# Sums of four squares written as a high and a low part and added by one-pass products, in three of the four openings of a decoder trunk

## The chip, the cores and the metric

The kernel runs on one core of a Trainium2 chip. The metric is the time of one execution on the device in microseconds. Three runs of the kernel before gave 2882.49, 2882.59 and 2882.88 us, so the median is 2882.59 us. The profiled execution is a fourth one; it took 2882.9 us by the same clock, of which 2881.1 us lie between its first and its last instruction (the span).

## The reference

It is a decoder trunk of two layers over 272 tokens (16 learned ones and 256 of the input) of width 2048, in float32. Every sub-layer is wrapped in two norms:

```
u = rmsnorm(h, pre_gain)
u = mixer(u)            # layer 0: sparse attention beside a gated delta rule; layer 1: retention
h = h + rmsnorm(u, post_gain)
u = swiglu(rmsnorm(h, ffn_pre_gain), w_gate, w_up, w_down)
h = h + rmsnorm(u, ffn_post_gain)
```

`rmsnorm(x)` is `x * rsqrt(mean(x*x) + 1e-6) * gain`, the mean taken over the 2048 channels of a token. There are eight norms, numbered 0 to 7 in the kernel. The even ones stand ahead of a large projection, the odd ones behind one. The change touches norms 2, 4 and 6.

## The kernel before, in words

Channels lie on the 128 partitions and in 16 chunks, tokens along the free axis, so `h` is 128 x 16 x 272. Norm 6 works on the 256 tokens behind the learned ones, the others here on all 272.

**Split products.** The kernel reaches float32 accuracy with one-pass products. Each weight and each activation is written as a high part (type fp32r) and a low part (the rest), and a tile of an output is 16 chunks times three products: high by high, low activation by high weight, high activation by low weight. ScalarE (ACT) writes the high parts (`w_hi`, `x_hi`), VectorE (DVE) subtracts them from the source to get the low parts (`w_lo`, `x_lo`; for norm 4 both lie in `ret_x`). SyncE (SP) issues the DMA loads of the weights. All matrix products go through the helper `mm`, which is why the profile gives nearly all of them line L647.

**An opening** is the start of the projection behind an even norm (stages up0, ret_in and up2 for norms 2, 4 and 6). The norm's factor is one number per token, so the products start on activations that aren't yet divided by the root; the root is applied when tiles leave PSUM. `fresh_three` computes the first three tiles together, chunk by chunk: for each chunk six products with `x_hi` and, one chunk later, three with `x_lo`. The fourth tile follows in `multiply`. TensorE waits for each chunk's `x_hi` and `x_lo` by semaphores, and for the first and second halves of each weight tile by `lo_ready`.

**What feeds it.** `h` itself is only finished in the opening. In `fill_x` of VectorE (L2280 and on) each pair of chunks goes through four steps in order: `x_low` of the pair (two instructions, L2333, from `h` and `x_hi`), `add_pair` of the pair after (L2348, one operand in PSUM), `scale_pair` (L2342, one operand in PSUM). Behind the last pair stand the first and second halves of the fourth tile's `w_lo` (L2325, 128x1024 each), the first half of the fifth tile's (L2258), and the reciprocal of the root (L2276). On ScalarE each pair gives two `x_hi` (L1599) and two squares (L1605); the squares of chunks 8 and on wait for `summed`, since their buffers are used again. The high part of the second half of the fourth tile's weights (L1552) waits until TensorE has passed the last pair of products of the second tile.

**The sum of squares.** In `square_fours` (L3122 and on) GpSimd (POOL) adds the squares in groups of four chunks, q = 0 to 3: chunk 0 + 1, chunk 2 + 3, and in `join` the two sums (three instructions, L3128). For q = 1 to 3 the join of the group before is held back until VectorE has written `x_lo` of chunk 4q + 1. The join of the last group has no such wait. TensorE adds the four results over partitions in `sum_four`: one float32 product with a matrix of ones, into one PSUM bank, behind chunks 7, 11 and 15 of `fresh_three` (sums 0, 1, 2) and behind chunk 3 of the fourth tile (sum 3). ScalarE then takes the root. The counters are `added` (POOL's additions), `summed` (sums done), `x_lo_ready`.

GpSimd's program from norm 1 on is: a running sum of squares for norm 1, half of a weight split, norm 2's fours, norm 3's sum, a weight split, norm 4's fours, the DMA of `rel`, the copy of the ones to fp32r (`ones_ret`, used in the retention), the retention's work, then norm 5's sum, a split and norm 6's fours.

The same high-and-low way of summing exists elsewhere in the kernel: in the delta rule (L3192 to L3203, with `ones_two`) and in the retention (L3294, L3296 and the products with `ones_ret`).

Of the kernel before, what the change touches and what calls it, by code (L numbers as in the profile page):

```python
# [28 lines left out]
ALU = mybir.AluOpType  # L29
AX = mybir.AxisListType  # L30

P = 128
D = 2048
META = 16
SEQ = 256
T = META + SEQ
KC = D // P
# [45 lines left out]

def added_after(norm, q, op):

    return 12 * (norm // 2) + 3 * q + op + 1  # L90
# [87 lines left out]
def trunk(nc, a, out):  # L178
    ctx = ExitStack()
    st = stage_table()  # L180
    with ctx:
        def sb(name, shape, dt=F32, c=ctx):
            return c.enter_context(nc.sbuf_tensor(name, shape, dt))

        def sem(name):
            return ctx.enter_context(nc.semaphore(name))
# [27 lines left out]
        ones = sb("ones", [P, P])  # L214
# [56 lines left out]
        with ExitStack() as second:  # L271
            with ExitStack() as whole:
                mid = sb("mid", [P, 64 * SEQ], F32R, whole)
# [20 lines left out]
            ones_ret = sb("ones_ret", [P, P], F32R, second)  # L294

        mid_hi = mid[:, 0:32 * SEQ]
        mid_lo = mid[:, 32 * SEQ:64 * SEQ]

        def mid_at(layer, low, j):

            if layer == 0:
                return 640 * j + (288 if low else 0)
            return (32 * SEQ + 32 if low else 64) + j * SEQ
# [15 lines left out]
        one_col = ones[:, 0:1]  # L319
# [53 lines left out]
        ps = ctx.enter_context(nc.psum_tensor("ps", [P, 8, 512], F32))  # L373
        BK_SUM, BK_D0, BK_D1, BK_0, BK_1, BK_2, BK_3 = 2, 2, 3, 4, 5, 6, 7
# [25 lines left out]
        x_lo_ready = sem("x_lo_ready")  # L400
        squared = sem("squared")
        added = sem("added")
        summed = sem("summed")
        rooted = sem("rooted")
        r_ready = sem("r_ready")
# [232 lines left out]
        def square_slot(norm, k):  # L638
            if norm == 0:
                return q_index[:, k % 8]  # L640
            return [ffn_g, ffn_m, k_rot, rot_a][k // 2 % 4][:, k % 2, FROM[norm]:T]
# [3 lines left out]
        def _(pe):  # L645
            def mm(o, lhs, rhs, start, stop):
                return nc.tensor.matmul(o, lhs, rhs, start=start, stop=stop)  # L647
# [69 lines left out]
            def fresh_pair(base):  # L717

                behind, t0 = 2, FROM[0]
                for k in range(KC + behind):  # L720
                    j = k - behind
                    if k < KC:
                        if k in (0, 4):
                            pe.wait_ge(first_lo, k // 2 + 1)
                        if k == 8:
                            pe.wait_ge(lo_ready, 2 * base + 2)
                        fresh_hi(0, k, t0)
                        half = fresh_lo(0, k, t0)
                        if k in (7, KC - 1):
                            half.then_inc(products, 1)  # L730
                    if k in (10, 14):
                        if k == 10:
                            pe.wait_ge(ones_in, 16)
                        sum_four(0, k // 4 - 2)
                    if j >= 0:
                        if j in (0, 4):
                            pe.wait_ge(first_lo, j // 2 + 2)
                        if j == 8:
                            pe.wait_ge(lo_ready, 2 * (base + 1) + 2)
                        last = multiply(ps[:, BK_1, t0:T], 1, j, 1, lambda _: x_hi[:, j, t0:T],  # L740
                                        lambda _: x_lo[:, j, t0:T], j == 0, j == KC - 1)
                last.then_inc(products, 2)

            def fresh_three(stage, norm, t0):
# [4 lines left out]
                for k in range(KC + 1):  # L749
                    j = k - 1  # L750
                    if k < KC:
                        if k == 8:
                            pe.wait_ge(lo_ready, 2 * base + 2)
                        fresh_hi(norm, k, t0)
                        if k % 8 == 0:
                            pe.wait_ge(lo_ready, 2 * (base + 1) + 1 + k // 8)
                        cut, high = slice(k * P, (k + 1) * P), x_of(x_hi, t0, norm)[:, k]
                        mm(second, w_hi[:, 1, cut], high, k == 0, False)
                        mm(second, w_lo[:, 1, cut], high, False, False)
                        if k == 0:  # L760
                            pe.wait_ge(third_lo_ready, 2 * THIRD.index(stage) + 2)
                        mm(third, third_hi[:, cut], high, k == 0, False)
                        mm(third, third_lo[:, cut], high, False, False)
                    if j >= 0:
                        fresh_lo(norm, j, t0)
                        cut, low = slice(j * P, (j + 1) * P), x_of(x_lo, t0, norm)[:, j]
                        pair = mm(second, w_hi[:, 1, cut], low, False, j == KC - 1)
                        if j == 7:
                            pair.then_inc(products, 1)
                        elif j == KC - 1:  # L770
                            pair.then_inc(products, 3)
                        last = mm(third, third_hi[:, cut], low, False, j == KC - 1)
                    if k in (7, 11, 15):
                        sum_four(norm, k // 4 - 1)
                last.then_inc(products, 2)

            def sum_four(norm, q):

                t0 = FROM[norm]
                if q == 0 and norm:  # L780
                    pe.wait_ge(r_ready, norm)
                pe.wait_ge(added, added_after(norm, q, 2))
                mm(ps[:, BK_SUM, t0:T], ones[:], square_slot(norm, 4 * q), q == 0, q == 3).then_inc(summed, 4)

            def sum_behind(norm):

                def behind(k):
                    if k == 3:
                        sum_four(norm, 3)
                return behind  # L790
# [2315 lines left out]
        def _(pool):  # L3106
            G = nc.gpsimd
# [15 lines left out]
            def square_fours(norm):  # L3123

                t0 = FROM[norm]

                def add(q, to, other):
                    G.tensor_tensor(square_slot(norm, 4 * q + to), square_slot(norm, 4 * q + to),  # L3128
                                    square_slot(norm, 4 * q + other), ALU.add).then_inc(added, 1)

                def join(q):
                    pool.wait_ge(added, added_after(norm, q, 1))
                    add(q, 0, 2)

                for q in range(4):
                    if q:

                        pool.wait_ge(x_lo_ready, KC * (norm // 2) + 4 * q + 2)
                        join(q - 1)
                    pool.wait_ge(squared, KC * norm + 4 * q + 2)  # L3140
                    add(q, 0, 1)
                    pool.wait_ge(squared, KC * norm + 4 * q + 4)
                    add(q, 2, 3)
                join(3)

            square_fours(0)

            for t in range(8):
# [95 lines left out]
            def square_sum(norm):  # L3244

                t0 = FROM[norm]

                def add(k, slot):
                    pool.wait_ge(squared, KC * norm + k + 1)
                    if isinstance(k, int) and k == 0:  # L3250
                        G.tensor_copy(sq_sum[:, t0:T], sq[:, slot, t0:T]).then_inc(summed, 1)
                    else:
                        pool.wait_ge(summed, KC * norm + k)
                        G.tensor_tensor(sq_sum[:, t0:T], sq_sum[:, t0:T], sq[:, slot, t0:T], ALU.add
                                        ).then_inc(summed, 1)

                add(0, 0)
                add(1, 1)
                with pool.Fori(1, KC // 2 - 1) as i:
                    for s in range(2):  # L3260
                        add(2 * i + s, s)

            def split_second(stage):

                piece = st[stage][0] + 1
                cut = slice(HALF_W, FULL)
                pool.wait_ge(hi_ready, 2 * piece + 2)
                pool.wait_ge(lo_ready, 2 * piece + 1)
                G.tensor_tensor(w_lo[:, 1, cut], raw[:, 1, cut], w_hi[:, 1, cut], ALU.subtract).then_inc(lo_ready, 1)

            square_sum(1)
            split_second("up0")
            square_fours(2)
            square_sum(3)
            split_second("ret_in")
            square_fours(4)
            _, sig, tile0 = st["ret_in"]
            pool.wait_ge(products, sig + 6)
            pool.dma_start(rel, a["rel"]).then_inc(rel_in, 16)
            G.tensor_copy(ones_ret[:], ones[:])  # L3280

            def ret_round(i):

# [116 lines left out]
```

## Time and profile before

| | value |
|---|---|
| median of three runs | 2882.59 us |
| profiled execution | 2882.9 us |
| its span | 2881.1 us |
| TensorE busy | 2854.4 us (99%) |
| VectorE busy | 1695.1 us (59%) |
| ScalarE busy | 1370.4 us (48%) |
| GpSimd busy | 244.0 us (8%) |
| opening of norm 2 | about 559 to 587 us |
| opening of norm 4 | about 1360 to 1387 us |
| opening of norm 6 | about 2147 to 2174 us |

The profile calls TensorE's products PE, its weight loads PEld. A row of the timeline has the start, the duration, the engine, the line, the operation, what is written and read, and how many like instructions were merged into it; brackets at its end give the idle time before it and who ended it. Products are pipelined, so what one costs TensorE is read from the distance of the starts and not from its duration.

### The profile page before, as it was taken

How to read it: one execution, taken by the hardware profiler on the slowest of the kernel's cores; microseconds unless marked ns; L12 is line 12 of the kernel's file. 1: busy time of each engine (PE TensorE's matmuls, PEld its weight loads, DVE VectorE, ACT ScalarE, POOL GpSimd, SP SyncE). 2: the span in 40 equal slices, each digit the busy share in tenths (PEclk: the TensorE clock that was granted, in tenths of full speed). 3: DMA queues.
4: the chain of work that ended last, by engine and by line, in shares of the span. 5: the costliest groups of instructions: out<-in, count | busy, mean ns of one | idle time of the engine just before them, and what ended most of it. 6: DMA issues, size and time to landing. Idle time of an engine off the chain costs nothing.

```text
span 2881.1 us, 58384 instructions
## 1 busy us (share of the span) xinstructions
PE 2854.4 (99%) x22720; PEld 2786.5 (97%) x22720; DVE 1695.1 (59%) x2402; ACT 1370.4 (48%) x1997; POOL 244.0 (8%) x273
## 2 busy tenths in 40 slices
PE   9999999999999999999999999999999999999998
PEld 8989999999999999999999999999999998899987
DVE  5887775755554455545655555555466556555555
ACT  5556665643343333345544444444454444344443
POOL 2222110300000000001211111110010000000000
PEclk9999999999999999999999999999999999999999
DMA  5222334444445544455344444444544555555554
GB/s 214 103 98 88 124 105 140 165 154 174 175 165 176 188 174 175 179 173 195 130 167 175 163 170 162 175 162 173 218 175 161 196 192 202 197 189 192 192 200 161
DMA packets 74823, 483.89 MB, mean 168 GB/s; under 512 B 8989, under 2 KB 9417, under 8 KB 24432
## 3 DMA queue, kind: packets, MB, share of 16 engines
q1 hardware_dynamic: 74528, 482.30, 47.2%
q8 instruction: 59, 0.97, 0.1%
q0 software_dynamic: 208, 0.39, 0.0%
q14 instruction: 28, 0.23, 0.0%
HBM read 480.41 MB, written 2.10 MB: 167 GB/s over the span
## 4 chain that ended last, share of the span: by engine, by line
PE 94%; DVE 4%; ACT 1%; issue 1%; DMA 0%; SPq 0%; POOL 0%; DVEq 0%; ACTq 0%
PE ps L647 93%; DVE w_lo L2258 0%; DVE w_lo L2406 0%; PE ps L1039 0%; DVE x_lo L2333 0%; DVE conv_acc L2435 0%; PE ps L1442 0%; DMA h<-in_x_t 0%; DVE ps L2342 0%; DVE h L2348 0%; DMA raw<-in_w_heads 0%; DVE bias L2537 0%; DVE r_pre L2276 0%; ACT w_hi L2002 0%; PE ps L947 0%
## 5 line engine op out<-in xcount | busy, mean ns | idle before, releaser
L2258 DVE TENSOR_TENSOR w_lo<-raw,w_hi 128x1024 fp32r<-128x1024 f32 (+2 forms) x885 | 1001.8, 1166 | 371.9 <-ACT w_hi L1520 357.8
L1520 ACT ACTIVATE w_hi<-raw 128x1024 fp32r<-128x1024 f32 (+2 forms) x835 | 822.9, 1012 | 519.3 <-PE ps L647 447.9
L647 PE MATMUL ps<-x_hi,w_hi 128*128 128x272 f32 (+1 forms) x3424 | 985.0, 288 | 7.4 <-ACT x_hi L1599 4.1
L647 PE MATMUL ps<-x_hi,w_lo 128*128 128x272 f32 (+1 forms) x3424 | 968.9, 283 | 0.2 <-DVE u L2672 0.2
L647 PE MATMUL ps<-x_lo,w_hi 128*128 128x272 f32 (+1 forms) x3424 | 963.8, 283 | 1.8 <-DVE x_lo L2333 1.8
L647 PEld LDWEIGHTS ps<-x_hi,w_hi 128*128 128x128 f32 x3424 | 645.4, 188 | 11.9 <-issue 4.6
L647 PEld LDWEIGHTS ps<-x_lo,w_hi 128*128 128x128 f32 x3424 | 643.3, 188 | 4.2 <-DVE x_lo L2333 2.9
L647 PEld LDWEIGHTS ps<-x_hi,w_lo 128*128 128x128 f32 x3424 | 642.3, 188 | 0.6 <-DVE u L2672 0.5
L647 PE MATMUL ps<-ret_x,w_hi 128*128 128x272 f32 (+1 forms) x3040 | 557.4, 284 | 1.5 <-ACT ret_x L1599 1.1
L647 PEld LDWEIGHTS ps<-ret_x,w_hi 128*128 128x128 f32 x3040 | 469.8, 188 | 2.4 <-ACT ret_x L1599 1.1
L647 PE MATMUL ps<-mid,w_hi 128*128 128x272 f32 (+1 forms) x2432 | 437.0, 282 | 0.0
L647 PE MATMUL ps<-ret_x,w_lo 128*128 128x272 f32 (+1 forms) x1520 | 429.7, 283 | 0.0
L647 PEld LDWEIGHTS ps<-mid,w_hi 128*128 128x128 f32 x2432 | 374.4, 188 | 0.0
L647 PE MATMUL ps<-mid,w_lo 128*128 128x272 f32 (+1 forms) x1216 | 342.7, 282 | 0.0
L647 PEld LDWEIGHTS ps<-ret_x,w_lo 128*128 128x128 f32 x1520 | 286.2, 188 | 0.0
L647 PEld LDWEIGHTS ps<-mid,w_lo 128*128 128x128 f32 x1216 | 228.0, 188 | 0.0
L647 PE MATMUL ps<-w_hi,mid 128*128 128x512 f32 x704 | 218.9, 392 | 0.0
L2145 ACT ACTIVATE mid<-ffn_m 128x272 f32 (+3 forms) x88 | 37.3, 424 | 342.0 <-DVE ffn_m L3001 342.0
L647 PEld LDWEIGHTS ps<-w_hi,mid 128*128 128x128 f32 x704 | 132.0, 188 | 29.5
L2159 ACT ACTIVATE ffn_g<-ffn_g 128x272 f32<-128x272 f32 (+1 forms) x88 | 37.3, 424 | 229.5 <-DVE ffn_g L2987 229.5
L647 PE MATMUL ps<-w_lo,mid 128*128 128x512 f32 x352 | 138.5, 393 | 0.0
L2997 DVE TENSOR_TENSOR ffn_m<-ps,r_pre 128x272 f32<-128x272 f32 (+1 forms) x88 | 38.0, 432 | 125.4 <-PE ps L647 125.4
(381 smaller groups left out, 2660.0 us busy)
## 6 DMA issues: line engine op xcount, KB each, us to landing
raw<-in_w_up SPq DMA_DIRECT2D x172, 1024.0 KB, 4.8
raw<-in_w_ret_in SPq DMA_DIRECT2D x94, 1024.0 KB, 4.8
raw<-in_w_down SPq DMA_DIRECT2D x64, 704.0 KB, 4.0
raw<-in_w_rows SPq DMA_DIRECT2D x44, 1024.0 KB, 4.8
raw<-in_w_heads SPq DMA_DIRECT2D x32, 1024.0 KB, 4.8
raw<-in_w_ret_out SPq DMA_DIRECT2D x32, 1024.0 KB, 4.8
raw<-in_w_mix_early SPq DMA_DIRECT2D x16, 768.0 KB, 4.3
raw<-in_w_latent SPq DMA_DIRECT2D x6, 1024.0 KB, 4.8
```

The lines of the kernel that those rows point to most:

```text
L647: return nc.tensor.matmul(o, lhs, rhs, start=start, stop=stop)
L1520: nc.scalar.activation(w_hi[:, piece % 2, cut], raw[:, piece % 2, cut], ACT.Copy).then_inc(hi_ready, count)
L2145: nc.scalar.activation(mid[:, bass.ds(mid_at(layer, False, j), w)], ffn_m[:, slot, 0:w], ACT.Copy).then_inc(mid_hi_ready, 1)
L2159: nc.scalar.activation(ffn_g[:, s, 0:w], ffn_g[:, s, 0:w], ACT.Silu).then_inc(gate_silu, 1)
L2258: V.tensor_tensor(w_lo[:, slot, cut], raw[:, slot, cut], w_hi[:, slot, cut], ALU.subtract).then_inc(lo_ready, count)
L2997: V.tensor_tensor(ffn_m[:, s, 0:w], ps[:, up_bank, t0:T], r_pre[:, t0:T], ALU.mult).then_inc(drained, 1)
```

## The change

For norms 2, 4 and 6 GpSimd writes two more instructions behind each join: the high part of the sum (`four_hi`, a multiplication by a column of ones into type fp32r) and the low part (`four_lo`, the sum less the high part). One pair of buffers serves all four groups, so from the second group on the high part waits until TensorE's sum of the group before is done. TensorE waits for both parts in place of the join (`fours_parted` in place of `added`), and adds two one-pass products in place of one float32 product. The copy of the ones to `ones_ret` moves ahead of norm 2's fours. Norm 0 stays as it was.

```diff
+def parted_after(norm, q, low):
+    return 8 * (norm // 2 - 1) + 2 * q + low + 1
@@
+        four_hi, four_lo = mid[:, 48 * SEQ:48 * SEQ + T], mid[:, 50 * SEQ:50 * SEQ + T]
@@
+        fours_parted = sem("fours_parted")
@@ sum_four (TensorE)
                 if q == 0 and norm:
                     pe.wait_ge(r_ready, norm)
-                pe.wait_ge(added, added_after(norm, q, 2))
-                mm(ps[:, BK_SUM, t0:T], ones[:], square_slot(norm, 4 * q), q == 0, q == 3).then_inc(summed, 4)
+                if norm == 0:
+                    pe.wait_ge(added, added_after(norm, q, 2))
+                    mm(ps[:, BK_SUM, t0:T], ones[:], square_slot(norm, 4 * q), q == 0, q == 3).then_inc(summed, 4)
+                    return
+                pe.wait_ge(fours_parted, parted_after(norm, q, 1))
+                mm(ps[:, BK_SUM, t0:T], ones_ret[:], four_hi[:, 0:T - t0], q == 0, False)
+                mm(ps[:, BK_SUM, t0:T], ones_ret[:], four_lo[:, 0:T - t0], False, q == 3
+                   ).then_inc(summed, 4)
@@ join, in square_fours (GpSimd)
                 def join(q):
                     pool.wait_ge(added, added_after(norm, q, 1))
                     add(q, 0, 2)
+                    if norm:
+                        total, high = square_slot(norm, 4 * q), four_hi[:, 0:T - t0]
+                        pool.wait_ge(added, added_after(norm, q, 2))
+                        if q:
+                            pool.wait_ge(summed, KC * norm + 4 * q)
+                        G.tensor_tensor(high, total, one_col.to_broadcast([P, T - t0]), ALU.mult
+                                        ).then_inc(fours_parted, 1)
+                        pool.wait_ge(fours_parted, parted_after(norm, q, 0))
+                        G.tensor_tensor(four_lo[:, 0:T - t0], total, high, ALU.subtract
+                                        ).then_inc(fours_parted, 1)
@@ GpSimd's program
             split_second("up0")
+            G.tensor_copy(ones_ret[:], ones[:])
             square_fours(2)
@@
             pool.dma_start(rel, a["rel"]).then_inc(rel_in, 16)
-            G.tensor_copy(ones_ret[:], ones[:])
```

## Rows read from the trace of the kernel before

**Rows 1.** The page: busy shares, TensorE's granted clock in 40 slices.
```profile
PE 2854.4 (99%) x22720; PEld 2786.5 (97%) x22720; DVE 1695.1 (59%) x2402; ACT 1370.4 (48%) x1997; POOL 244.0 (8%) x273
PEclk9999999999999999999999999999999999999999
```

**Rows 2.** TensorE's waits: norm 2's opening, then a later one in norm 4's.
```profile
564.83 0.39 PE L647 MATMUL ps<-x_hi,w_hi 128*128 128x272 f32 x1 [1.08 <-ACT x_hi L1599]
...
1393.82 0.49 PE L647 MATMUL ps<-ret_x,w_hi 128*128 128x272 f32 x2 [0.41 <-DVE k_rot L3076]
```

**Rows 3.** Timeline of TensorE, norm 2: sum 0 and two products behind it.
```profile
569.49 0.62 PE L647 MATMUL ps<-ffn_g,ones 128*128 128x272 f32 x2
569.75 0.49 PE L647 MATMUL ps<-x_hi,w_hi 128*128 128x272 f32 x1
570.08 0.29 PE L647 MATMUL ps<-x_hi,w_lo 128*128 128x272 f32 x1
570.20 0.29 PE L647 MATMUL ps<-x_hi,w_hi 128*128 128x272 f32 x1
```

**Rows 4.** Timeline of TensorE: a pair of one-pass products, in the retention.
```profile
1434.44 0.41 PE L647 MATMUL ps<-ret_x,ones_ret 128*128 128x256 f32 x2
1434.68 0.40 PE L647 MATMUL ps<-ret_x,w_hi 128*128 128x256 f32 x2
```

**Rows 5.** Timeline of TensorE: sum 2 of norm 2, sum 3 of norms 2 and 6.
```profile
579.46 0.62 PE L647 MATMUL ps<-ffn_g,ones 128*128 128x272 f32 x2
...
581.79 0.62 PE L647 MATMUL ps<-k_rot,ones 128*128 128x272 f32 x2
...
2167.88 0.59 PE L647 MATMUL ps<-k_rot,ones 128*128 128x256 f32 x2
```

**Rows 6.** GpSimd's high and low parts elsewhere: nanoseconds, minimum/median/maximum.
```profile
L3201 POOL TENSOR_TENSOR third_hi<-u,ones x7: 639/640/1857, 155.4 to 422.2; 128x272 fp32r<-128x272 f32 x7
L3203 POOL TENSOR_TENSOR third_hi<-u,third_hi x7: 663/663/727, 157.3 to 422.9; 128x272 fp32r<-128x272 f32 x7
L3296 POOL TENSOR_TENSOR ret_x<-ret_sq,ret_x x8: 741/741/743, 1433.1 to 1960.3; 128x256 fp32r<-128x256 f32 x8
```

**Rows 7.** Timeline of GpSimd, norm 2: first addition, joins 0 and 2, last addition, join 3.
```profile
560.35 0.96 POOL L3128 TENSOR_TENSOR ffn_g<-ffn_g 128x272 f32<-128x272 f32 x1 [1.32 <-ACT ffn_g L1605]
...
565.95 0.76 POOL L3128 TENSOR_TENSOR ffn_g<-ffn_g,ffn_m 128x272 f32<-128x272 f32 x1 [2.66 <-DVE x_lo L2333]
...
575.49 0.78 POOL L3128 TENSOR_TENSOR ffn_g<-ffn_g,ffn_m 128x272 f32<-128x272 f32 x1 [1.72 <-DVE x_lo L2333]
...
577.74 1.75 POOL L3128 TENSOR_TENSOR rot_a<-rot_a 128x272 f32<-128x272 f32 x1 [0.73 <-ACT rot_a L1605]
579.57 0.76 POOL L3128 TENSOR_TENSOR k_rot<-k_rot,rot_a 128x272 f32<-128x272 f32 x1
```

**Rows 8.** Timeline of VectorE, norm 2: chunks 6 and 7, then the end.
```profile
567.24 0.92 DVE L2333 SCALAR_TENSOR_TENSOR x_lo<-h,gains,x_hi 128x272 fp32r<-128x272 f32 x2
...
576.63 1.09 DVE L2333 SCALAR_TENSOR_TENSOR x_lo<-h,gains,x_hi 128x272 fp32r<-128x272 f32 x2 [0.59 <-ACT x_hi L1599]
577.64 1.21 DVE L2325 TENSOR_TENSOR w_lo<-fourth_raw,w_hi 128x1024 fp32r<-128x1024 f32 x1
581.46 1.23 DVE L2325 TENSOR_TENSOR w_lo<-fourth_raw,w_hi 128x1024 fp32r<-128x1024 f32 x1 [2.60 <-ACT w_hi L1552]
582.60 1.22 DVE L2258 TENSOR_TENSOR w_lo<-raw,w_hi 128x1024 fp32r<-128x1024 f32 x1
```

**Rows 9.** GpSimd and VectorE side by side in the retention.
```profile
1389.56 1.64 POOL L3287 TENSOR_TENSOR q_rot<-rot_a,q_rot 128x256 f32<-128x256 f32 x1 [7.49 <-DVE q_rot L3076]
1391.16 1.72 POOL L3288 TENSOR_TENSOR q_rot<-rot_a,q_rot 128x256 f32<-128x256 f32 x1
...
1389.39 2.89 DVE L2258 TENSOR_TENSOR w_lo<-raw,w_hi 128x1024 fp32r<-128x1024 f32 x2
```

**Rows 10.** GpSimd's DMA of `rel`: size, microseconds from issue to landing.
```profile
h_rows<-in_rel POOLq DMA_DIRECT2D x1, 232.0 KB, 3.1
```

## The prediction, as put on record before the change was run

> **What bounds the kernel now.** I read the page first. TensorE is busy 99% of the span at the full granted clock, GpSimd 8% [rows 1]. So what TensorE is spared comes off the time, and what it is made to wait goes on it. Then I listed its waits. In norm 2's opening there is one of 1.08 us, for `x_hi` of chunk 4, long before the sums that change; behind the openings one matters here, 0.41 us in norm 4's, for a drained tile [rows 2]. Then I laid the engines' timelines side by side in the three openings. They have the same order of instructions three times; the rows shown are norm 2's, and I walk that one.
>
> The profiled execution took 2882.9 us (span 2881.1, 1.8 around it). Its time is 0.3 above the median of 2882.59; I add my sum to the median.
>
> **TensorE's part.** Sum 0 starts at 569.49, the product behind the next one at 570.08, and plain products follow each other by 0.12 to 0.13 [rows 3]. So a float32 sum costs 0.59 - 0.125 = 0.465 us. A pair of one-pass products is in the retention: from its start to the next, 0.24 us for 256 columns [rows 4], taken as 0.25 for 272. Saved: 0.21 in each of 8 sums, and in norm 6's four some 0.19 (its sum's row is 0.03 shorter [rows 5]): together **-2.4 us**. This is the lower bound of everything else, since nothing else is removed.
>
> **GpSimd's part.** Each of 12 joins gets a high part, 0.64 us undisturbed, and a low part, 0.66 to 0.74 [rows 6]; with 0.08 us for each wait on its own result (join 3 starts 0.08 behind the addition that ended at 579.49 [rows 7]) that is 1.5 us. Sums 0 to 2 can carry it: join 0 ends at 566.71, sum 0 is at 569.49; join 2 ends at 576.27, sum 2 is at 579.46 [rows 3, 5, 7]. Sum 3 is another matter. Join 3 ends at 580.33 and TensorE comes at 581.79 [rows 5, 7], 1.46 us later, and at 581.16 once three sums are cheaper. Ahead of join 3 now stand three more pairs of instructions, of which the third is in the chain: join 2 is held to 575.49 by `x_lo` of chunk 13, and from there GpSimd runs nearly without a pause.
>
> **The port.** What decides is how long GpSimd's instructions take there. The addition at 577.74 took 1.75 us, its neighbours 0.76 [rows 7]. VectorE ran a 128x1024 split from 577.64 to 578.85 [rows 8], and the addition ended 0.64 behind it. The retention shows the rule in full: two such splits start at 1389.39, GpSimd's instruction of 1389.56 ends at 1391.20, the next at 1392.88, and the two splits together take 2.89 us instead of some 2.35 [rows 9]. First split to 1390.53, GpSimd 0.66, second split to 1392.28, GpSimd 0.60. So a GpSimd instruction and a VectorE instruction with two operands in SBUF exclude each other, one instruction at a time, in turn. The rows of `x_lo` (two operands in SBUF) obey it; the ones with an operand in PSUM don't: join 0, at 565.95, took its plain 0.76 us beside one. From these rows, a held GpSimd instruction ends 0.64 (addition) or 0.60 (low part) behind its rival, I take 0.52 for the high part; a held `x_lo` ends 0.30, a held split 1.08 behind.
>
> The Trainium skill speaks here against the change: its GPSIMD Engine Reference (section 1, Specifications) has GpSimd's SBUF interfaces shared with VectorE, with contention where VectorE's instruction has two SBUF inputs. The trace agrees, and adds the turns.
>
> **The walk, norm 2.** Join 0 to 566.72, high part to 567.44. `x_lo` of chunk 6 is issued at 567.24 [rows 8], held, done 567.74; low part to 568.34; `x_lo` 7 to 568.64 instead of 568.16. VectorE is 0.5 late; `h`, and so `x_hi` of chunk 8, too: TensorE waits 0.1 to 0.2 and has lost what sum 0 saved. The same at join 1, another 0.1 late or less, with sum 1's gain spent. Join 2 is released near 576.05. Its high part ends at 577.54, `x_lo` 14 at 577.84, low part 578.44, `x_lo` 15 578.74 (before 577.72), the first of the last two additions 579.38, the split that ran at 577.64 ends at 580.46, second addition 581.10. Sum 2 at TensorE is at 579.5 as before; the fourth tile starts some 0.2 late.
>
> Join 3: 581.18 to 581.94. The next split was issued at 581.46, behind a `w_hi` that ScalarE writes once TensorE is past sum 2, so it keeps its place; it waits for the join and ends at 583.02. High part to 583.54. The fifth tile's split, issued behind it [rows 8], to 584.62. Low part to **585.22**. TensorE wants sum 3 at some 582.0, starts at 585.27 and is through at 585.52, where before it was at 581.79 + 0.465 = 582.25: **+3.3 us**, which holds the savings of all four sums.
>
> The same walk gives +4.0 in norm 4, since its first low part comes just ahead of `x_lo` 6 and holds both chunks, so that TensorE waits 0.8 at chunk 8 and keeps that delay; less the 0.4 us wait behind it [rows 2], which vanishes (root and drains are late by less than TensorE): +3.6. In norm 6 the sum is over at 2171.7, before at 2167.88 + 0.43 = 2168.3 [rows 5]: +3.4. **Sum: +10.3 us.**
>
> **Bounds of the walk.** If VectorE isn't pushed back before join 3, join 3 is at 580.33 to 581.08, the high part done by 581.80, ahead of the split; that ends at 582.88, low part 583.48, sum over at 583.78: +1.5 per opening, 4.1 in all after the 0.4. If join 3 falls just behind the split's start, the end moves by half a microsecond: +3.9 per opening, +11.5 in all. I take the walk, because the turns reproduce each stretched row to 0.05 us.
>
> **The rest.** The copy of the ones moves into the 1.32 us in which GpSimd waited ahead of norm 2's fours [rows 7]: nothing. The DMA of `rel` goes out some 5 us later and lands 3.1 us after [rows 10], still ahead of its reader in the retention, which is behind the late root: nothing; without that cover the two or three microseconds would be ScalarE's. The wait on `summed` is met each time: sum 2 is over near 580, its buffers are written at 583. The root waits for sum 3 but stood behind two of ScalarE's splits before, so it is late by less than TensorE itself, and the drains that it releases keep their place. No queue of SyncE is passed.
>
> **Rivals.**
> A, *late, but little*: GpSimd's high part of sum 3 gets in ahead of the split. For it: join 3 is ahead of it now by 0.8 us. Against: the walk eats that. +4.1: 2886.7. Chance 0.17.
> B, *all hidden*: the low part of sum 3 is there by 581.2. Against: even with undisturbed durations the eight instructions from join 2's release at 575.49 on, 6.1 us with their waits, end at 581.6. -2.4: 2880.2, the other side of the zero. It decides only if GpSimd gets through them in 5.7 us. Chance 0.06.
> C, *the clock falls too*: a wait of 3.3 us between full stretches isn't in this trace, the granted clock is full in all 40 slices [rows 1]; the longest wait of these openings, 1.08 us [rows 2], left it full. If it halved for the rest of the fourth tile (36 products by 0.125 = 4.5 us), each opening would cost 4.5 more, +23.8: 2906. Chance 0.05. The Trainium skill bears on it (TensorE: Matmul & The Clock Gate, Why this matters for your kernels): it advises against idle gaps between bursts of products, since the clock drops behind them. By it the time would be C's 2906; the trace agrees as far as waits of 1.08 us go, which left the clock full, and shows none of 3 us here.
> D, *one opening of three as in A*, or a pair of one-pass products as dear as the float32 one (+2.4): between 2888 and 2896, inside my range.
>
> **The numbers.** This kernel's runs can tell about 0.2%, 5.8 us, from no change. Forecast 2882.6 + 10.3 = **2892.9** (with D, chance 0.72; its own range 2888.5 to 2895.5). A and B lie within 0.2%, together 0.23, and 0.02 of the walk's low end too; C counts as slower. Slower 0.73, same 0.25, faster 0.02 (only beyond what is removed). The range takes in most of A: 2885.5 to 2895.5, leaving out B, C and the tails, 0.2.
>
> **What would show it.** TensorE's first one-pass product of sum 3 waits 3 us or more on GpSimd in each of three openings; GpSimd's high and low parts there take 1.5 us each and more; pairs of `x_lo` at chunks 6 and 10 take 1.4 us instead of 0.92; the three splits behind them are 1 us or more late; norm 4's wait of 0.41 is gone. Wrong if sum 3's wait is under 2 us (A), absent (B), or if the clock's row shows less than 9 in slice 9, 20 or 31 (C).

## The result, and the profile after

Five runs of the changed kernel gave 2897.00 to 2899.05 us, median 2897.68; the kernel before gave a median of 2882.53 beside them. The ratio is 1.0052, with a 95% interval of 1.0042 to 1.0063: **15.1 us slower**, where 10.3 were forecast. The profiled execution took 2897.7 us (span 2895.8, 14.7 more than before). Helpers moved down, so L647 is now L654, `x_lo` is L2346, the two kinds of `w_lo` L2338 and L2271, GpSimd's additions L3141; its high part is L3152 and its low part L3155.

The page, busy shares and the clock in 40 slices:

```profile
PE 2858.5 (99%) x22720; PEld 2789.1 (96%) x22720; DVE 1705.4 (59%) x2402; ACT 1370.9 (47%) x1997; POOL 267.7 (9%) x297
...
PEclk9999999999999999999999999999999999999999
```

Against [rows 1] almost nothing has moved: GpSimd has its 24 instructions and 24 us more. TensorE's waits, grouped by who released them (us in total, times, longest), say where the time is:

```profile
PE ps L654 <- POOL mid L3155: 8.8, 3, 3.0
PE ps L654 <- ACT x_hi L1612: 4.8, 8, 1.1
PE ps L654 <- ACT ret_x L1612: 2.1, 3, 1.0
```

The first line is new: one wait in each opening for the low part of sum 3. In the same view of before, the next two were 4.1 (6 times) and 1.1 (twice): 1.7 us more, for the high parts of activations. Norm 2 has one more such wait, of 0.85 us, ahead of chunk 12, and norm 4 one of 0.97 us, ahead of chunk 8 (right behind sum 0); in norm 6 none of this size is new. The wait for `k_rot` of [rows 2] is gone. Norm 2's opening, TensorE's sums and waits, then norm 4's sum 0 and the wait behind it:

```profile
569.48 0.41 PE L654 MATMUL ps<-mid,ones_ret 128*128 128x272 f32 x2
574.61 0.41 PE L654 MATMUL ps<-mid,ones_ret 128*128 128x272 f32 x2
575.86 0.39 PE L654 MATMUL ps<-x_hi,w_hi 128*128 128x272 f32 x1 [0.85 <-ACT x_hi L1612]
580.51 0.41 PE L654 MATMUL ps<-mid,ones_ret 128*128 128x272 f32 x2
581.56 0.36 PE L654 MATMUL ps<-x_hi,w_hi 128*128 128x272 f32 x1 [0.26 <-DVE w_lo L2338]
586.22 0.51 PE L654 MATMUL ps<-mid,ones_ret 128*128 128x272 f32 x2 [2.92 <-POOL mid L3155]
...
1374.17 0.41 PE L654 MATMUL ps<-mid,ones_ret 128*128 128x272 f32 x2
1375.55 0.36 PE L654 MATMUL ps<-ret_x,w_hi 128*128 128x272 f32 x1 [0.97 <-ACT ret_x L1612]
```

Sum 0 of norm 2 stands where it stood [rows 3]; sum 2 is 1.05 us late and sum 3 is 4.43 late [rows 5]. GpSimd in the same stretch (joins 1, 2 and 3 with what follows them):

```profile
571.04 0.77 POOL L3141 TENSOR_TENSOR k_rot<-k_rot,rot_a 128x272 f32<-128x272 f32 x1 [0.99 <-DVE x_lo L2346]
571.89 0.64 POOL L3152 TENSOR_TENSOR mid<-k_rot,ones 128x272 fp32r<-128x272 f32 x1
572.61 0.77 POOL L3155 TENSOR_TENSOR mid<-k_rot,mid 128x272 fp32r<-128x272 f32 x1
573.34 0.98 POOL L3141 TENSOR_TENSOR ffn_g<-ffn_g 128x272 f32<-128x272 f32 x1
...
576.98 0.77 POOL L3141 TENSOR_TENSOR ffn_g<-ffn_g,ffn_m 128x272 f32<-128x272 f32 x1 [1.73 <-DVE x_lo L2346]
...
580.29 1.74 POOL L3141 TENSOR_TENSOR rot_a<-rot_a 128x272 f32<-128x272 f32 x1
582.12 0.78 POOL L3141 TENSOR_TENSOR k_rot<-k_rot,rot_a 128x272 f32<-128x272 f32 x1
582.97 1.50 POOL L3152 TENSOR_TENSOR mid<-k_rot,ones 128x272 fp32r<-128x272 f32 x1
584.55 1.62 POOL L3155 TENSOR_TENSOR mid<-k_rot,mid 128x272 fp32r<-128x272 f32 x1
```

And VectorE, chunks 6 and 7, then 10 and 11, then the splits:

```profile
567.25 1.44 DVE L2346 SCALAR_TENSOR_TENSOR x_lo<-h,gains,x_hi 128x272 fp32r<-128x272 f32 x2
...
572.11 0.73 DVE L2355 TENSOR_TENSOR ps<-u,ps 128x544 f32<-128x544 f32 x1 [0.51 <-DVE h L2361]
572.74 1.88 DVE L2346 SCALAR_TENSOR_TENSOR x_lo<-h,gains,x_hi 128x272 fp32r<-128x272 f32 x2
...
582.31 1.67 DVE L2338 TENSOR_TENSOR w_lo<-fourth_raw,w_hi 128x1024 fp32r<-128x1024 f32 x1 [0.90 <-ACT w_hi L1565]
583.90 1.66 DVE L2271 TENSOR_TENSOR w_lo<-raw,w_hi 128x1024 fp32r<-128x1024 f32 x1
```

The turns are there. The split issued at 582.31 waits for join 3 (to 582.90) and ends at 583.98; the high part waits for it and ends at 584.47; the next split waits for that and ends at 585.56; the low part waits for that and ends at 586.17. Only then does TensorE start. Undisturbed, high and low part take 0.64 and 0.77 (571.89 and 572.61); here they take 1.50 and 1.62.

At sum 3 the other openings show the same turns, and one thing more. Norm 4's last sum and the products behind it, then the stretches of the windows view (window and its length, then busy time and count of PE, PEld, DVE, ACT and POOL; then the granted clock, DMA's share, GB/s):

```profile
1390.95 0.82 PE L654 MATMUL ps<-mid,ones_ret 128*128 128x272 f32 x2 [2.98 <-POOL mid L3155]
1391.57 0.65 PE L654 MATMUL ps<-ret_x,w_hi 128*128 128x272 f32 x2
1392.02 0.43 PE L654 MATMUL ps<-ret_x,w_lo 128*128 128x272 f32 x1
...
1394.06 0.31 PE L654 MATMUL ps<-ret_x,w_lo 128*128 128x272 f32 x1
```

```profile
586.00:589.00 3.00, 2.78 (x22) 2.78 (x23) 1.70 (x1) 1.77 (x2) 0.17 (x1) 1.00 0.00 0
1390.00:1391.00 1.00, 0.05 (x1) 0.06 (x1) 0.28 (x1) 0.00 (x0) 1.00 (x2) 0.84 0.00 0
1391.00:1394.00 3.00, 3.00 (x13) 3.00 (x14) 1.67 (x1) 0.49 (x1) 0.46 (x1) 0.50 0.34 85
1394.00:1395.00 1.00, 1.00 (x10) 1.00 (x9) 0.96 (x3) 0.51 (x1) 0.00 (x0) 0.95 0.00 0
...
2181.00:2184.00 3.00, 2.92 (x19) 2.92 (x20) 1.83 (x2) 1.76 (x2) 0.03 (x1) 0.76 0.00 0
2184.00:2186.00 2.00, 2.00 (x11) 2.00 (x11) 1.97 (x4) 1.37 (x2) 0.00 (x0) 0.50 0.00 0
```

The granted clock is at its lower level (1.2 instead of 2.4 GHz) for 0.32 + 3 + 0.1 = 3.4 us behind the wait of 2.98 us in norm 4, and again for 1.4 + 2 = 3.4 us in norm 6, where the fall comes about 1.5 us after the products are back from a wait of 2.93 us. Behind norm 2's wait of 2.92 us it stays full. A stretch of 3.4 us at half speed does the work of 1.7 us, so each costs **1.7 us**, 3.4 in this execution. The clock's row of the page can't show it: a slice there is 72 us.

**Where the 14.7 us are**, by the first product of each opening. Norm 4's first product comes at 1364.22, before at 1359.90; norm 6's at 2156.22, before at 2146.80:

```profile
1364.22 0.36 PE L654 MATMUL ps<-ret_x,w_hi 128*128 128x272 f32 x1 [0.22 <-ACT ret_x L1612]
...
2156.22 0.36 PE L654 MATMUL ps<-x_hi,w_hi 128*128 128x256 f32 x1 [0.33 <-ACT x_hi L1612]
...
2181.08 0.51 PE L654 MATMUL ps<-mid,ones_ret 128*128 128x256 f32 x2 [2.93 <-POOL mid L3155]
```

So norm 2 cost 4.3, norm 4 5.1 and norm 6 the remaining 5.3. Less the clock, 4.3 + 3.4 + 3.6 = 11.3 us.

### The profile page after: what moved, and what is told of

The parts are those of the page before. It is cut to its first block, busy times and chain, and to the rows that moved or that the text cites. A ratio compares the mean times of both kernels' runs of the same rounds, so it can differ in the third digit from the quotient of the medians.

```text
span 2895.8 us, 58408 instructions
## 1 busy us (share of the span) xinstructions
PE 2858.5 (99%) x22720; PEld 2789.1 (96%) x22720; DVE 1705.4 (59%) x2402; ACT 1370.9 (47%) x1997; POOL 267.7 (9%) x297
## 4 chain that ended last, share of the span: by engine, by line
PE 92%; DVE 3%; POOL 2%; ACT 1%; issue 1%; DMA 0%; SPq 0%; POOLq 0%; DVEq 0%; ACTq 0%
PE ps L654 91%; POOL mid L3155 0%; POOL mid L3152 0%; POOL k_rot L3141 0%; DVE w_lo L2419 0%; DVE x_lo L2346 0%; DVE ps L2355 0%; DVE w_lo L2271 0%; PE ps L1052 0%; POOL rot_a L3141 0%; POOL ffn_g L3141 0%; DVE conv_acc L2448 0%; PE ps L1455 0%; DMA h<-in_x_t 0%; DVE h L2361 0%
## 5 line engine op out<-in xcount | busy, mean ns | idle before, releaser
L2271 DVE TENSOR_TENSOR w_lo<-raw,w_hi 128x1024 fp32r<-128x1024 f32 (+2 forms) x885 | 1003.0, 1168 | 369.6 <-ACT w_hi L1533 355.6
L654 PE MATMUL ps<-x_hi,w_hi 128*128 128x272 f32 (+1 forms) x3424 | 985.3, 288 | 8.8 <-ACT x_hi L1612 4.8
L654 PE MATMUL ps<-x_hi,w_lo 128*128 128x272 f32 (+1 forms) x3424 | 969.7, 284 | 0.2 <-DVE u L2685 0.2
L654 PE MATMUL ps<-x_lo,w_hi 128*128 128x272 f32 (+1 forms) x3424 | 964.3, 283 | 1.5 <-DVE x_lo L2346 1.5
L654 PEld LDWEIGHTS ps<-x_hi,w_hi 128*128 128x128 f32 x3424 | 646.1, 189 | 14.4 <-issue 5.7
L654 PEld LDWEIGHTS ps<-x_lo,w_hi 128*128 128x128 f32 x3424 | 643.9, 189 | 3.8 <-DVE x_lo L2346 2.8
L654 PEld LDWEIGHTS ps<-x_hi,w_lo 128*128 128x128 f32 x3424 | 643.1, 188 | 0.5 <-DVE u L2685 0.5
L654 PE MATMUL ps<-ret_x,w_hi 128*128 128x272 f32 (+1 forms) x3040 | 557.9, 284 | 2.3 <-ACT ret_x L1612 2.1
L654 PEld LDWEIGHTS ps<-ret_x,w_hi 128*128 128x128 f32 x3040 | 470.7, 189 | 3.3 <-issue 1.5
L654 PE MATMUL ps<-mid,w_hi 128*128 128x272 f32 (+1 forms) x2432 | 437.0, 282 | 0.0
L654 PE MATMUL ps<-ret_x,w_lo 128*128 128x272 f32 (+1 forms) x1520 | 430.1, 283 | 0.0
L654 PEld LDWEIGHTS ps<-mid,w_hi 128*128 128x128 f32 x2432 | 374.3, 188 | 0.0
L654 PE MATMUL ps<-mid,w_lo 128*128 128x272 f32 (+1 forms) x1216 | 342.7, 282 | 0.0
L654 PEld LDWEIGHTS ps<-ret_x,w_lo 128*128 128x128 f32 x1520 | 286.8, 189 | 0.0
L654 PEld LDWEIGHTS ps<-mid,w_lo 128*128 128x128 f32 x1216 | 228.0, 188 | 0.0
L654 PE MATMUL ps<-w_hi,mid 128*128 128x512 f32 x704 | 218.9, 392 | 0.0
L654 PEld LDWEIGHTS ps<-w_hi,mid 128*128 128x128 f32 x704 | 132.0, 188 | 29.5
L654 PE MATMUL ps<-w_lo,mid 128*128 128x512 f32 x352 | 138.5, 393 | 0.0
```

Source lines behind the costliest of these rows:

```text
L2271: V.tensor_tensor(w_lo[:, slot, cut], raw[:, slot, cut], w_hi[:, slot, cut], ALU.subtract).then_inc(lo_ready, count)
```

## The experiments

All ratios are to the kernel before on the same chip, whose medians there were 2882.53 (e1 to e4), 2882.83 (e5 to e8) and 2882.84 us (e9, e10). The 95% intervals reach some 0.1% (2.6 us) to either side, so those of e2, e4, e6, e8 and e9 reach "no change". The repeats lie closer together than that: e4's slowest run (2881.18) is under the fastest of the kernel before (2882.01), and the lowest runs of e6 and e8 (2883.80 and 2884.94) are over its median beside them. Differences under about 0.5 us are not read. In the cuts of the edits the counting of the semaphores, which follows each edit, is left out. My theory: the turns between GpSimd and VectorE push sum 3's parts behind the splits. Rivals: GpSimd simply has too many instructions, the new wait or the one-pass products are what costs, or the clock does.

### e1: only sums 0 to 2 parted

```diff
@@ sum_four
-                if norm == 0:
+                if norm == 0 or q == 3:
@@ join
-                    if norm:
+                    if norm and q < 3:
```

> High and low parts and one-pass products for sums 0, 1 and 2 only; sum 3 of each opening as before. Theory (turns at the port, chain in front of sum 3): VectorE's x_lo of chunks 6, 7, 10, 11 are pushed as in the changed kernel (1.44 and 1.88 us a pair in norm 2's opening in place of 0.92 and 0.91), so TensorE is still late at chunk 12 and the fourth tile still begins 1.3 us late (581.56 in place of 580.29); join 3 ends near 582.9, just ahead of TensorE's 583.1, so no wait of more than 0.2 us on GpSimd, and the clock stays full. Sum over three openings: +1.3, +0.8, +0.7, so +2.8 us (2885.3). Rival (the whole loss is the wait at sum 3 and the clock behind it; the parts ahead cost TensorE nothing): three sums cheaper in three openings, -1.8 us (2880.7).

Measured 2885.86 us, ratio 1.0011 (1.0002 to 1.002): **+3.3**. TensorE waits 0.85 us at chunk 12, as in the changed kernel, and join 3 starts 12.6 us behind sum 0 (581.53, 568.90), as there: the parts of sum 3 have no share in join 3's lateness. The theory said +2.8, the rival -1.8.

### e2: only sum 3 parted

```diff
-                if norm == 0:
+                if norm == 0 or q < 3:
@@ join
-                    if norm:
+                    if norm and q == 3:
```

> High and low part and one-pass products for sum 3 only; sums 0 to 2 as before. Theory (turns): VectorE is not pushed before join 3; join 3 to 581.08, high part 581.80, VectorE's split behind it to 582.88, low part 583.48, so TensorE waits 1.7 us at sum 3 and each opening costs +1.5, less the 0.4 wait that vanishes in norm 4's: +4.1 us (2886.7); the clock stays full behind waits of 1.7 us. Rival (only the length of the chain counts, no exclusion): low part at 582.6, +0.6 per opening, +1.5 in all (2884.1).

Measured 2882.59 us, ratio 1.0 (0.9991 to 1.0009): **no change**; the expectation missed. GpSimd, then VectorE's split:

```profile
579.04 0.77 POOL L3141 TENSOR_TENSOR k_rot<-k_rot,rot_a 128x272 f32<-128x272 f32 x1
579.89 0.64 POOL L3150 TENSOR_TENSOR mid<-k_rot,ones 128x272 fp32r<-128x272 f32 x1
580.61 0.77 POOL L3153 TENSOR_TENSOR mid<-k_rot,mid 128x272 fp32r<-128x272 f32 x1
```

```profile
580.90 1.56 DVE L2338 TENSOR_TENSOR w_lo<-fourth_raw,w_hi 128x1024 fp32r<-128x1024 f32 x1 [2.57 <-ACT w_hi L1565]
```

Join 3 ends at 579.81, both its parts are done at 581.38, and TensorE takes the sum at 581.43. This time the split waits for GpSimd (it ends at 582.46, 1.08 behind the low part) and not the other way round. The bound had read 580.33, the *end* of join 3 in [rows 7], as its start. Sum 3's parts alone cost nothing; they cost when earlier pairs have pushed join 3 into the splits.

### e3: GpSimd writes the parts of groups 0 to 2, TensorE doesn't use them

The float32 products stay; TensorE waits for the parts as in e1.

```diff
@@ sum_four
-                if norm == 0:
+                if norm >= 0:
+                    if norm and q < 3:
+                        pe.wait_ge(fours_parted, parted_after(norm, q, 1))
                     pe.wait_ge(added, added_after(norm, q, 2))
@@ join
-                    if norm:
+                    if norm and q < 3:
```

> GpSimd writes the parts of groups 0, 1 and 2, but TensorE adds the sum itself by one float32 product as before (it waits for the parts, which are early). Theory (turns): the loss of the parts ahead of sum 3 is VectorE's, not TensorE's, and TensorE is bound by x_hi of chunks 8 and 12 and by the split of the fourth tile; so nearly the time of the kernel with the cheaper sums, at most 0.6 us more per opening: +3 to +4.5 us (2885.5 to 2887). Rival (GpSimd's added work is free until sum 3): +0.0 (2882.5).

Measured 2885.87 us, ratio 1.0011 (1.0002 to 1.002): **+3.3**, the same as e1. In norm 2 TensorE waits 0.65 us at chunk 12 instead of e1's 0.85: what a cheaper sum spares it, it waits longer for the next chunk.

### e4: the one-pass products alone

GpSimd writes no parts; the twelve pairs of products add two buffers of constants, so the sum of squares is left out. Time only.

```diff
-                pe.wait_ge(fours_parted, parted_after(norm, q, 1))
+                pe.wait_ge(added, added_after(norm, q, 2))
+                pe.wait_ge(fours_parted, norm)
@@ join
-                    if norm:
+                    if False:
```

> TensorE's side alone: all 12 sums as pairs of one-pass products, with GpSimd's parts left out (the buffers hold ones, written once ahead of each opening, so the root is that of a constant). Theory (rows of the retention): 0.21 or 0.19 us saved per sum, 2.4 in all (2880.1). Rival (a pair costs what a float32 product costs): +0.0 (2882.5).

Measured 2880.61 us, ratio 0.9993 (0.9984 to 1.0002): **-1.9** of the 2.4. The wait for `k_rot` in norm 4 is 0.54 us instead of 0.41. In norm 2 sum 3 starts 11.72 us behind sum 0 (580.96, 569.24) instead of 12.30, so each of the three sums between saves 0.19 us: the products are nearly as cheap as forecast (0.21).

### e5: TensorE kept busy while it waits

The changed kernel, with 12 float32 products into an unused bank ahead of sum 3's wait.

```diff
                     if k == 3:
+                        for _ in range(12):
+                            mm(ps[:, BK_D1, 0:P], ones[:], ident[:], True, True)
                         sum_four(norm, 3)
```

> The changed kernel, and behind chunk 3 of the fourth tile, ahead of the wait for sum 3, twelve float32 products of 128 columns into an unused bank (some 2.6 us of TensorE's time, which lies in the wait of 2.9 to 3.0). Theory (the clock fell because TensorE stood idle): the granted clock stays full in all three openings, TensorE starts sum 3 at the same place behind GpSimd, and the time falls by the 3.4 us that two half-speed stretches cost: 2894.3 us, and the runs no longer differ by steps of 1.7. Rival (the clock fell for another reason): 2897.7 as before.

Measured 2894.51 us, ratio 1.0041 (1.0028 to 1.0054): **+11.7**, 3.4 less than the changed kernel's +15.1. Norm 2, and the sums of norms 4 and 6:

```profile
582.73 2.84 PE L654 MATMUL ps<-ident,ones 128*128 128x128 f32 x24
...
585.82 0.52 PE L654 MATMUL ps<-mid,ones_ret 128*128 128x272 f32 x2 [0.25 <-POOL mid L3157]
...
1390.57 0.51 PE L654 MATMUL ps<-mid,ones_ret 128*128 128x272 f32 x2 [0.31 <-POOL mid L3157]
...
2179.31 0.51 PE L654 MATMUL ps<-mid,ones_ret 128*128 128x256 f32 x2 [0.26 <-POOL mid L3157]
```

The sum starts neither earlier nor later for the added work (in norm 2, 16.75 us behind sum 0 here and 16.74 in the changed kernel), and the products behind it run at the full clock. The halved clock is shown to be the changed kernel's second cost, and to hang on TensorE being idle.

### e6: fills in place of the parts

GpSimd's two instructions are fills of 600 columns, about as long (0.60 us); the high and low parts are left out.

```diff
-                        G.tensor_tensor(high, total, one_col.to_broadcast([P, T - t0]), ALU.mult
-                                        ).then_inc(fours_parted, 1)
+                        G.memset(mid[:, 48 * SEQ:48 * SEQ + 600].bitcast(F32), 1.0).then_inc(fours_parted, 1)
```

(and the same for the low part, whose buffer moves on to make room)

> The changed kernel with each high and low part replaced by a fill of 600 columns with ones (some 0.6 us each, no input read; the sum is that of constants). Same waits, same count of instructions. Theory (what excludes the engines is GpSimd's reading of SBUF beside VectorE's second input): fills neither hold x_lo nor are held, pairs of x_lo take 0.92 us again, join 3 comes at some 580.2, the second fill ends near 582.3, TensorE waits under 0.8 us at sum 3: +0.6 to +1.0 us against before (2883.3). Rival (the chain's length alone, or any instruction of GpSimd, does it): within 2 us of the changed kernel (2895.7 or more).

Measured 2884.02 us, ratio 1.0005 (0.9996 to 1.0014): **+1.2**. GpSimd, then VectorE:

```profile
576.45 0.60 POOL L3152 MEMSET mid<- 128x600 f32 x1
577.10 0.60 POOL L3154 MEMSET mid<- 128x600 f32 x1
577.67 1.78 POOL L3141 TENSOR_TENSOR k_rot<-k_rot 128x272 f32<-128x272 f32 x1
...
580.26 0.77 POOL L3141 TENSOR_TENSOR k_rot<-k_rot,rot_a 128x272 f32<-128x272 f32 x1
```

```profile
576.76 0.92 DVE L2346 SCALAR_TENSOR_TENSOR x_lo<-h,gains,x_hi 128x272 fp32r<-128x272 f32 x2 [0.59 <-ACT x_hi L1612]
577.60 1.22 DVE L2338 TENSOR_TENSOR w_lo<-fourth_raw,w_hi 128x1024 fp32r<-128x1024 f32 x1
```

The fill of 577.10 and the `x_lo` of 576.76 run at once, neither longer for it, while the addition right behind is held by the split. The same instruction slots, without the turns, cost a tenth: TensorE waits 0.70 to 0.94 us for the last fill of each opening, 2.5 in all, most of it paid for by the cheaper products. That rules out the count of instructions and the new waits as the main cause. They have a part in it: join 3 (580.26) starts 11.18 us behind sum 0, where it was 10.08 in the kernel before and 12.64 in the changed one, so 1.1 us of its 2.6 come from the length of the chain. The fills are some 0.2 us a pair shorter than the parts: over four pairs at most 0.8 us per opening, 2.4 in all, far from ten.

### e7: sum 3 behind chunk 11 of the fourth tile

```diff
-                    if k == 3:
+                    if k == 11:
                         sum_four(norm, 3)
```

> The changed kernel with TensorE's sum 3 behind chunk 11 of the fourth tile in place of chunk 3, 3.0 us later. Theory: VectorE is pushed as before, so 2.8 to 3.3 us stay; the wait on GpSimd nearly vanishes (under 0.3 us), the clock stays full; the root is as late as in the changed kernel, so TensorE waits 0 to 1 us for drained tiles at the sixth tile: 2885.5 to 2888 us. Rival (the late root costs what the late sum did): over 2892.

Measured 2892.24 us, ratio 1.0032 (1.002 to 1.0044): +9.4, 5.7 less than the changed kernel's +15.1, where 10 to 12 less were expected. The theory missed; the rival's "over 2892" is what came. The waits for GpSimd are nearly gone (0.22 us is left, in norm 6). In their place:

```profile
PE ps L654 <- DVE k_rot L3089: 2.4, 1, 2.4
...
PE ps L654 <- DVE ffn_m L3010: 1.9, 2, 1.1
```

The root comes behind the late sum, the drains behind the root, and TensorE waits for the banks. Behind the 2.4 us in norm 4 the clock halves as well (0.57 over 1400 to 1404). The wait has moved to its next owner.

### e8: a running total

Built on the kernel before (the core of the edit is shown): GpSimd adds the four groups up itself (three more additions per opening), TensorE makes one float32 product behind chunk 7 of the fourth tile.

```diff
+                    G.tensor_tensor(sq_sum[:, t0:T], sq_sum[:, t0:T], square_slot(norm, 4 * q), ALU.add
+                                    ).then_inc(added, 1)
```

> Built on the kernel before: GpSimd adds the four group sums into one running total (three more additions per opening, no parts), and TensorE makes one float32 product of it behind chunk 7 of the fourth tile in place of four spread over the opening. The additions come behind joins 1 and 2, in stretches where VectorE has an operand in PSUM, and behind join 3. Theory: three float32 products less per opening, 1.4 us each opening, of which TensorE can use some 1.05 because x_hi of chunks 12 and 14 then bind it: -3.2 us against before (2879.4), and under 0.3 us of wait for the total. Rival (additions push VectorE as the parts do): +0.5 to +2 us.

Measured 2885.52 us, ratio 1.0009 (1.0 to 1.0018): **+2.7**, a miss. Three of four products are spared, and one addition for each of the last three groups is enough to lose that and more: the pair of `x_lo` at 571.74 takes 1.90 us, TensorE waits 1.11 us at chunk 12 and 0.66 us for a split. Not all of it is the additions: the sum also comes four chunks later, and the wait for `k_rot` in norm 4 is 1.1 us instead of 0.41.

### e9: only sum 3 parted, two chunks later

```diff
-                    if k == 3:
+                    if k == 5:
```

(on top of e2)

> Only sum 3 is parted, and TensorE takes it behind chunk 5 of the fourth tile instead of chunk 3. Theory (in e2_last_one the parts of sum 3 were there 0.2 us behind TensorE's arrival, at no held chunk): the sum then starts without any wait and saves 0.21 us in each of three openings, and the root, which comes 1 us later, still reaches the drained tiles in two of the three: 2882.6 - 0.6 = 2882.0 us, less by up to 0.6 if k_rot in norm 4 isn't later. Rival (the root is what the drained tiles wait for): TensorE's wait for k_rot in norm 4, 0.41 us in the kernel before, grows by up to 1 us: 2882.6 to 2883.2.

Measured 2882.54 us, ratio 1.0 (0.9991 to 1.0009), 0.3 under the kernel before: nothing that its runs can tell. The wait for `k_rot` grew from 0.41 to 0.77 us and took half of the 0.6 spared.

### e10: the pair behind join 2 left out

```diff
-                if norm == 0:
+                if norm == 0 or q == 2:
@@ join
-                    if norm:
+                    if norm and q != 2:
```

> The changed kernel with the pair behind join 2 left to a float32 product; groups 0, 1 and 3 are parted. Theory (it is the pairs' sum that pushes join 3 into the splits, and the third is 1.5 us of it, in the chain from join 2 on): join 3 starts near 580.7 in norm 2 and its high part gets in ahead of the split or just behind it; TensorE's wait at sum 3 is 0 to 1.5 us instead of 2.9, the one at chunk 12 (0.85 us, from the held x_lo of chunks 10 and 11) stays: 2884.5 to 2888.5 us, clock full. Rival (the delay of the first two pairs, through VectorE, is enough by itself): join 3 past 581.5, its low part behind both splits, a wait of over 2.5 us, 2892 and more.

Measured 2888.98 us, ratio 1.0021 (1.0012 to 1.0031): **+6.1**, half a microsecond over the theory's range and far under the rival's 2892.

```profile
580.87 0.78 POOL L3141 TENSOR_TENSOR k_rot<-k_rot,rot_a 128x272 f32<-128x272 f32 x1
581.72 0.64 POOL L3152 TENSOR_TENSOR mid<-k_rot,ones 128x272 fp32r<-128x272 f32 x1
582.44 1.74 POOL L3155 TENSOR_TENSOR mid<-k_rot,mid 128x272 fp32r<-128x272 f32 x1
```

Join 3 starts at 580.87, its high part gets in ahead of the splits (the first is issued at 582.34), and the low part waits for one of them. TensorE waits 1.39 to 1.50 us instead of 2.92 to 2.98, and the clock stays full.

### Together

Executions start their openings some tenths apart, so join 3 is given here from the start of sum 0 of norm 2 (569.48 in the changed kernel, 568.95 in e2, 569.08 in e6, 569.32 in e10, 569.07 in e5):

| version | join 3 starts | splits ahead of the low part | against before |
|---|---|---|---|
| before [rows 3, 7] | +10.08 | (none written) | |
| e2, sum 3 only | +10.09 | none | +0.1 |
| e6, fills in place of the parts | +11.18 | (not held) | +1.2 |
| e10, without the third pair | +11.55 | one | +6.1 |
| changed kernel | +12.64 | two | +15.1 |
| e5, the same at full clock | +12.64 | two | +11.7 |

The 15.1 us are 1.2 for the instructions as such, less what the cheaper products save (e6), 10.5 for their turns with VectorE (e5 less e6) and 3.4 for the clock (the changed kernel less e5).

## Why the prediction was right and wrong

- **Sign and mechanism: right.** A wait of about 3 us on GpSimd's low part in each of three openings, at the place named, made by the turns (2.92 to 2.98 against 3.27 in the walk, which put TensorE's arrival at 582.0 and the start at 585.27).
- **TensorE's saving, -2.4: nearly right** (e4 -1.9, with 0.13 more lost to `k_rot`), and right that the savings of the sums ahead are spent by the fourth tile (e1 against e3, the same time).
- **Step that failed, the walk of norm 2 at join 1.** It said "the same at join 1, another 0.1 late or less". It let VectorE's delay from chunks 6 and 7 be absorbed; in the trace the 0.51 us of idle time ahead of the scaling (572.11) stay as they were before, so `x_lo` of chunk 10 is issued 0.5 us late, at 572.74, next to join 1's low part; both `x_lo` of the pair are held by GpSimd (1.88 us, where 1.40 was taken), and TensorE waits 0.85 us at chunk 12, where the walk had 0.1 to 0.2 us at such a place. So sum 2, forecast at 579.5 as before, comes at 580.51, and the fourth tile, forecast 0.2 late, starts 1.3 late. Join 3 starts at 582.12 instead of 581.18, and sum 3 at 586.22 instead of 585.27. Norm 2 cost 4.3 instead of 3.3.
- **The walks of norms 4 and 6: right.** Without the clock they came to 3.4 and 3.6, forecast 3.6 and 3.4, and the traces show the steps that were forecast. In norm 4 the first low part holds both `x_lo` of chunks 6 and 7 and TensorE waits 0.97 us at chunk 8, forecast 0.8. In norm 6 the pairs of `x_lo` at chunks 6 and 10 take 1.37 and 1.36 us, as the walk had them. So without the clock the sum is 11.3 instead of 10.3, all of the difference from norm 2.
- **Step that failed, rival C.** The clock was given 0.05 and a price of 4.5 us per opening. It fell behind two of three waits, and each fall cost 1.7 us. The 0.05 rested on a wait of 1.08 us that had left the clock full [rows 2], which says nothing of one of 3 us; the rule of the Trainium skill (TensorE: Matmul & The Clock Gate, Why this matters for your kernels), which advises against idle gaps because the clock drops behind them, was the better guide. The trace after agrees with it in norms 4 and 6 (a granted clock of 0.50), and not in norm 2 (1.00). These 3.4 us are what carried the time out of the range, which took C as all or nothing: e5, with the clock full, lies inside it (2894.51). The price was mis-sized because it let the half clock last for the rest of the tile; it lasted 3.4 us.
- **The bound of rival A** started join 3 at 580.33, which is the end of join 3 before and not its start [rows 7]. With no pair ahead the start stays at +10.08 and both parts get in ahead of the split, at no cost (e2); with three pairs ahead and VectorE not pushed it is +11.18 (e6, with fills), 580.67 in the time of [rows 7], so the figure was near by luck. Its price for one split ahead of the low part, 1.5 us per opening, is what e10 shows: waits of 1.39 to 1.50 us. The slip is at the low end of the range and has no share in the miss.
- **The clock test in the prediction** (a digit under 9 in slices 9, 20 or 31) could not have found this: 1.7 us of a slice of 72 us is 2%.
- `rel`'s DMA, the copy of the ones and the wait on `summed`: none releases a wait of TensorE after.

Left open: why norm 2's wait of 2.92 us left the clock full and norm 6's of 2.93 didn't. The run of 2899.05 us had a mean clock of 0.997 where the others had 0.998, and is some 1.5 us longer, as a third such stretch would make it; there is no trace of it, so this is not shown.

## What to carry to other kernels

Before work moves to GpSimd in a stretch where VectorE runs instructions with two operands in SBUF, lay the two timelines side by side: each of GpSimd's instructions that meets one of these waits until it is done, so ask which long one stands ahead of the *last* result that TensorE needs, and mind that delays of earlier groups decide it. A saving on TensorE ahead of a chunk that comes at another engine's pace is no saving. When a wait of some microseconds is forecast on an otherwise full TensorE, give a halved clock behind it a real chance, and look for it in stretches of a few microseconds, not in the page's slices.

## What the runs showed of the hardware that was not expected

- GpSimd's fills take no part in the turns: 0.60 us beside an `x_lo` of 0.92, neither longer (e6). Its additions and parts do: 0.78 and 0.64 us become 1.74 and 1.50.
- The granted clock halved for 3.4 us behind waits of 2.98, 2.93 and (e7) 2.35 us, and not behind waits of 2.92 (norm 2) and 1.5 us (e10). In norm 4 it fell while TensorE still waited, in norm 6 about 1.5 us after it was back at work.
- Twelve float32 products of 128 columns in the gap kept the clock full at no cost (e5).
